# A recurrence, a post norm and two mixer layers re-ordered on one core

## The reference

```python
# first block
h = rms_norm(x, g_pre) * (1 + scale) + shift
q, k, v, g_att, u, g_lru, merge = split(h @ w_in)
y_a = (dilated_attention(q, k, v) * silu(g_att)) @ w_pa
u = causal_depthwise_conv(u, conv_w, conv_b)
# rg_lru: per feature, over the tokens t
r, i = sigmoid(u @ w_rg + b_rg), sigmoid(u @ w_ig + b_ig)   # 64 x 64 blocks
log_a = -8 * r * softplus(-lru_lambda); a = exp(log_a)
h_t = a * h_{t-1} + sqrt(-expm1(2 * log_a)) * (i * u)
y_b = (h * silu(g_lru)) @ w_pb
out = (gate_a * y_a + gate_b * y_b) @ w_o
x = x + gate * rms_norm(out, g_post)
# second block, for l in 0, 1: context ctx (256 tokens) and x (512 tokens)
hc, hx = modulate(rms_norm(ctx)), modulate(rms_norm(x))
a_val, a_gate, q, k, v, u, sv, bg, cg, xin = split(hx @ w_in[l])   # 10 parts of 256
y_a = silu(layer_norm(depthwise_conv31(a_val * sigmoid(a_gate))))
y_b = rms_norm((softmax(q1 k1) - lam * softmax(q2 k2)) v)   # 4 heads, keys of ctx and x
y_c = gelu(u) * (w_s @ layer_norm(gelu(sv)))
y_d = bg * depthwise_conv3(cg * xin)
x = x + gate * concat(y_a, y_b, y_c, y_d) @ w_out[l]
x = x + gate * relu(modulate(rms_norm(x)) @ w1)**2 @ w2
# layer 0 does all of this for ctx too
```

## Time and profile before

| | us |
|---|---|
| median of 3 runs (2217.7 to 2224.73) | 2219.04 |
| the profiled execution's own time | 2221.63 |
| its span in the trace | 2219.8 |
| TensorE busy | 2067.8 (93%) |
| VectorE busy | 1271.8 (57%) |
| ScalarE busy | 797.8 (36%) |
| GpSimd busy | 88.4 (4%) |
| TensorE's mean granted clock | 0.977 |

### The profile page before, as it was taken

How to read it: one execution, slowest core, us unless ns; L and a number is a source line. 1 busy time by engine, 2 the same in 40 slices (tenths; PEclk the granted TensorE clock), 3 DMA queues, 4 the chain that set the end, 5 groups by cost and what they waited for, 6 DMA issues and landing times.

```text
span 2219.8 us, 26153 instructions
## 1 busy us (share of the span) xinstructions
PE 2067.8 (93%) x11000; PEld 1756.8 (79%) x11000; DVE 1271.8 (57%) x1674; ACT 797.8 (36%) x1105; POOL 88.4 (4%) x89
## 2 busy tenths in 40 slices
PE   5999999998999898899999999999888889999998
PEld 5978777776777787788888888888777677888886
DVE  7465765756755695736645455464558555343343
ACT  4433334475243255424212121131525533232231
POOL 0000000000050000011000000001200000000001
PEclk9999999999998999999999999999999999999999
DMA  8533523522422531112323332232342212222222
GB/s 296 204 142 114 202 83 116 182 88 97 188 78 94 159 82 61 67 58 95 126 95 114 107 114 102 102 136 86 114 140 77 76 67 76 95 95 95 95 97 75
DMA packets 52821, 249.17 MB, mean 112 GB/s; under 512 B 6016, under 2 KB 10256, under 8 KB 34272
## 3 DMA queue, kind: packets, MB, share of 16 engines
q1 hardware_dynamic: 50816, 242.41, 31.6%
q0 software_dynamic: 592, 2.46, 0.3%
q10 hardware_dynamic: 1296, 2.63, 0.3%
HBM read 235.41 MB, written 12.06 MB: 111 GB/s over the span
## 4 chain that ended last, share of the span: by engine, by line
PE 74%; DVE 12%; ACT 7%; issue 4%; DMA 2%; POOL 0%; SPq 0%; ACTq 0%; DVEq 0%; POOLq 0%
PE banks L1707 62%; ACT whi_f L1829 2%; DVE small L1265 1%; DVE wlo_f L2011 1%; PE banks L607 1%; PE banks L616 1%; PE banks L1730 1%; PE banks L1731 1%; PE banks L1732 1%; PE banks L496 1%; DVE aconv L1177 1%; DVE prob L1285 1%; DMA mvr<-in_mst 1%; DVE mvr L2031 1%; PE banks L487 1%
## 5 line engine op out<-in xcount | busy, mean ns | idle before, releaser
L1707 PE MATMUL banks<-hxh,whi_f 128*128 128x512 f32 x1440 | 587.2, 408 | 47.8 <-DVE hxl L2050 14.9
L1707 PE MATMUL banks<-hxh,wlo_f 128*128 128x512 f32 x1440 | 571.2, 397 | 0.0
L1707 PE MATMUL banks<-hxl,whi_f 128*128 128x512 f32 x1440 | 570.6, 396 | 0.0
L2011 DVE TENSOR_TENSOR wlo_f<-raw_f,whi_f 128x2048 fp32r<-128x2048 f32 x133 | 305.7, 2298 | 215.0 <-ACT whi_f L1829 214.9
L1829 ACT ACTIVATE whi_f<-raw_f 128x2048 fp32r<-128x2048 f32 x133 | 253.8, 1908 | 310.3 <-PE banks L1707 291.7
L1707 PEld LDWEIGHTS banks<-hxh,whi_f 128*128 128x128 f32 x1440 | 275.1, 191 | 112.6 <-issue 42.9
L1707 PEld LDWEIGHTS banks<-hxh,wlo_f 128*128 128x128 f32 x1440 | 274.7, 191 | 60.1
L1707 PEld LDWEIGHTS banks<-hxl,whi_f 128*128 128x128 f32 x1440 | 275.3, 191 | 58.1 <-issue 1.9
L1707 PE MATMUL banks<-fxh,whi_f 128*128 128x512 f32 x512 | 202.5, 396 | 2.2 <-DVE cT L1395 1.1
L1395 DVE SCALAR_TENSOR_TENSOR xT<-banks,small,xT 128x512 f32<-128x512 f32 x80 | 59.5, 750 | 252.4 <-PE banks L1707 252.3
L1707 PE MATMUL banks<-fxh,wlo_f 128*128 128x512 f32 x512 | 201.3, 393 | 0.0
(11 more groups left out here) (316 smaller groups left out, 3170.9 us busy)
## 6 DMA issues: line engine op xcount, KB each, us to landing
raw_f<-in_wst SPq DMA_DIRECT2D x133, 1024.0 KB, 4.9
mvr<-in_mst SPq DMA_DIRECT2D x120, 512.0 KB, 5.8
stack<-qk_parts SPq DMA_DIRECT2D x48, 192.0 KB, 6.9
x_kept<-xT SPq DMA_DIRECT2D x2, 2048.0 KB, 8.6
raw_f<-in_wst SPq DMA_DIRECT2D x8, 384.0 KB, 6.0
xT<-x_kept SPq DMA_DIRECT2D x2, 1536.0 KB, 8.8
qk_parts<-qk_h SPq DMA_DIRECT2D x3, 768.0 KB, 3.4
qk_parts<-qk_l SPq DMA_DIRECT2D x3, 768.0 KB, 4.9
```

Source lines behind the costliest of these rows:

```text
L1707: last = pe.matmul(o, w[:, k, c, :], r[part][:, k, :], start=(k == order[0] and w is wh and part == 0), stop=(k == order[-1] and w is wl))
L2011: dve.tensor_tensor(wlo[r][:], raw[r][:], whi[n % 2 if n > N_FIRST else n][:].bitcast(F32), ALU.subtract).then_inc(w_lo, 1)
```

## The change

Recurrence: the result of tile j is written straight into `uc`, in the new token order, so that `bh` and `bl` are plain copies; they are made one pass later, `bh` between exp and sqrt, `bl` (`recurrence_low`) before VectorE waits for sqrt. Post norm: the split of chunk C_L + 1 moves behind the norm's root and inverse; GpSimd's adds for `n_mix[0]` go, and TensorE sums each of the eight squared tiles by itself (`tile_sums`), among the 32 context steps. Layers: the first stack of each layer is filled from `qk_h` and `qk_l` in SBUF by 16 transfers instead of from DRAM; `Y_ORDER`, the places of the rotations, of the convolution's taps and of several splits move; the context norm of layer 1 is begun in the last feed-forward chunk; accumulators are waited for one at a time; the y tiles wait tile by tile for their buffer (`hx_free`).

```diff
-Y_ORDER = (4, 5, 6, 7, 0, 1, 2, 3)
+Y_ORDER = (4, 5, 0, 1, 6, 7, 2, 3)
...
+                        if i == 0:
                             pe.wait_ge(acc_free[c], n)
-                        if k == 0 and c == 0:
-                            pe.wait_ge(acc_free[1], n)
-                        last = step(n, j % 2, k, c, own, at=lambda r: ctx_acc[:, c, :] if r[2] else acc[:, c, 0:T])
+                        if i == 0 and c == 0 and l == 0:
+                            pe.wait_ge(ctx_out, j - 5)
+                        last = step(n, j % 2, k, c, own, order, lambda r: ctx_acc[:, c, :] if r[2] else acc[:, c, 0:T])
...
-                 between={(0, 0): lambda: o_turned(0), (0, 2): lambda: o_turned(1)}, order=Y_ORDER)
+                 between={(0, 7): lambda: o_turned(0), (0, 2): lambda: o_turned(1)}, order=Y_ORDER)
...
+                if j > 2:
+                    high(j - 3)
...
-                    for k in range(KT):
-                        act.wait_ge(acc_free[k % 2], base - 4 + k // 2 + 1)
-                        norm_square(SC, cT, nsqc, k)
-                if j == 1 and l:
-                    norm_root(SC, c_mix[1])
+                    for k in range(4):
+                        norm_high(SC, c_mix[1], hch, k, mod_shift(0, k, 1))
...
-            square_o(0)
             upto(p.mean)
+            act.wait_ge(m_cen, l + 1)
+            act.activation(sqm[:, :, 0:wx], yca[:, :, 0:wx], ACT.Square).then_inc(m_sq, 1)
             act.wait_ge(sv_cen, l + 1)
...
-            act.wait_ge(m_cen, l + 1)
-            act.activation(sqm[:, :, 0:wx], yca[:, :, 0:wx], ACT.Square).then_inc(m_sq, 1)
+            square_o(0)
...
+                if i < 4:
+                    act.wait_ge(hx_free, 4 * l + i + 1)
+                else:
+                    act.wait_ge(acc_ready[1], base + N_WIN)
...
-            act.wait_ge(acc_ready[1], base + N_WIN)
             last = p.units - 1
-            if not two:
-                scaled(last)
-                square_o(1)
...
+            y_high(5)
             split(base + N_WIN + 1)
+            y_high(6)
+            y_high(7)
...
+                            if two:
+                                norm_square(SC, cT, nsqm, 2 * i + c)
...
+                for c in range(2):
+                    act.wait_ge(acc_free[c], n + 1)
+                    norm_square(SC, cT, nsqm, KT - 2 + c)
...
+                norm_root(SC, c_mix[1])
...
+                if j == 0 and l:
+                    for k in range(KT - 1):
+                        norm_scale(SC, c_mix[1], cT, k, coef[0][:, 2 * k + 1:2 * k + 2])
                 if j == 2:
-                    if l:
-                        for k in range(KT):
-                            conv(1)
-                            norm_scale(SC, c_mix[1], cT, k, coef[0][:, 2 * k + 1:2 * k + 2])
-                    else:
-                        conv(13)
+                    conv(13 if two else 11)
                 if j > 2:
                     rotate(j - 3)
+                    if j == 4:
+                        split(n + 1)
                     low(j - 3)
-                    conv(7 if two else 9)
-                split(n + 2)
+                    conv((7, 9)[j - 3] if two else 11)
+                if j != 3:
+                    split(n + 2)
...
+                    due[0] = n + 2
+            due = [None]
+            def weights_due():
+                if due[0] is not None:
+                    split(due[0])
+                due[0] = None
...
                 maxima(v0)
                 for v in range(v0, v1):
                     if v + 1 < v1:
                         maxima(v + 1)
+                    weights_due()
                     combine(v)
-                    conv(count)
+                    if v0 == 0:
+                        conv(3 if v < more else 2)
                     if v in late:
                         late[v]()
-            run(0, p.cut, 3)
+            run(0, p.cut, CONV_STEPS - taps[0] - 2 * p.cut)
...
+            dve.wait_ge(gelus, 2 * l + 1)
+            link(dve.tensor_scalar(sv_mean[:, 0:nj], sv_sum[:, 0:nj], 1.0 / GW, None, ALU.mult))
+            dve.tensor_tensor(svn[:, 0:nj, :], svn[:, 0:nj, :], by_row(sv_mean), ALU.subtract).then_inc(sv_cen, 1)
+            weights_due()
...
-            for i in range(4):
-                y_low(i)
+            y_low(0)
+            y_low(1)
+            upto(89)
+            y_low(2)
+            y_low(3)
...
+            y_low(5)
             split(base + N_WIN + 1)
+            y_low(6)
+            y_low(7)
...
+                if b == 0:
                     sync.wait_ge(x_kept, 16 * (l + 1))
                     sync.wait_ge(SX.low, KT * (n_mix[l].m + 1))
                     sync.wait_ge(SC.scaled, KT * (c_mix[l].m + 1))
+                for part, src in enumerate((qk_h[b], qk_l[b])):
+                    sync.wait_ge((qk_hi, qk_lo)[part], 2 * l + b + 1)
+                    for i in range(4):
+                        if STACKED[b][i] == part:
+                            for e in range(2):
+                                sync.dma_start(stack[0][32 * i:32 * i + 32, 2 * b + e, 0:w].bitcast(F32),
+                                               src[32 * e:32 * e + 32, 0, 0:w].bitcast(F32)).then_inc(stacked[0], 16)
+                    sync.dma_start(qk_dram[l][2 * b + part, :, :, 0:w].rearrange("c p t -> p c t"), src[:, :, 0:w].bitcast(F32)
+                                   ).then_inc(qk_kept[b], 16)
...
-                    load_stack(l, 0)
...
             add_square(SX, n_post, nsq, 6)
-            add_squares(SX, n_mix[0], nsq2)
             for l in range(L2):
                 if l:
-                    add_squares(SX, n_mix[1], nsq3)
-                    add_squares(SC, c_mix[1], nsqc)
+                    for k in range(1, KT - 1):
+                        add_square(SX, n_mix[1], nsq3, k)
+                        add_square(SC, c_mix[1], nsqm, k)
...
+            def tile_sums(k):
+                pe.wait_ge(SX.squared, KT * n_mix[0].i + k + 1)
+                for j in range(SX.nj):
+                    last = pe.matmul(SX.st[:, j:j + 1], nsq2[:, k, j * P:(j + 1) * P], ones[:, 0:1],
+                                     start=(k == 0 and j == 0), stop=(k == KT - 1), skip_group_check=True)
+                if k == KT - 1:
+                    last.then_inc(SX.summed, 1)
...
-                for k in range(KT):
+            sums_at = (13, 15, 16, 18, 19, 21, 22, 24)
+            for s in range(4 * KT):
+                j, c, k = s // (2 * KT), s // KT % 2, s % KT
+                if s % (2 * KT) == 0:
+                    weights(C_L + j)
+                if s in (0, KT):
+                    pe.wait_ge(acc_free[c], C_L)
+                if s == 3:
+                    norm_spread(SX, n_post)
+                if s in sums_at:
+                    tile_sums(sums_at.index(s))
+                if s == 27:
+                    norm_spread(SX, n_mix[0])
+                if j == 0:
                     wait_low(SC, c_mix[0], k)
-                    step(C_L, 0, k, c, [(*hc, T, TC)])
-                    if (c, k) == (0, 1):
...
-            norm_sums(SX, n_mix[0], nsq2)
-            norm_spread(SX, n_mix[0])
+                step(C_L + j, j, k, c, [(*hc, T + TC * j, TC)])
...
+                if j:
+                    act.wait_ge(lru_out, j)
                 act.activation(a_, r_, ACT.Exp, scale=nsp[:, j:j + 1]).then_inc(lru_ta, 1)
                 if j + 2 < N_MRG:
                     act.dma_start(wgate[:, j % 2, :], gst[j + 2]).then_inc(g_loaded[j % 2], 16)
+                if j:
+                    act.activation(tile(bh, j - 1), tile(uc, j - 1), ACT.Copy).then_inc(lru_hi, 1)
                 act.wait_ge(lru_z, j + 1)
                 act.activation(z_, z_, ACT.Sqrt).then_inc(lru_sq, 1)
-                act.wait_ge(lru_out, j + 1)
-                act.activation(by_residue(tile(bh, j)), in_order(x_), ACT.Copy).then_inc(lru_hi, 1)
             merged(N_MRG - 1)
+            act.wait_ge(lru_out, N_MRG)
+            act.activation(tile(bh, N_MRG - 1), tile(uc, N_MRG - 1), ACT.Copy).then_inc(lru_hi, 1)
             for j in range(N_PA):
...
+            def recurrence_low(j):
+                dve.wait_ge(lru_hi, j + 1)
+                dve.tensor_tensor(tile(bl, j), tile(uc, j), tile(bh, j).bitcast(F32), ALU.subtract
+                                  ).then_inc(lru_lo, 1)
             for j in range(N_MRG):
                 if j:
                     split(C_MRG + j + 1)
+                dve.wait_ge(lru_ri, 2 * j + 2)
+                link(dve.tensor_tensor(x_, i_, tile(uc, j), ALU.mult))
                 dve.wait_ge(lru_ta, 2 * j + 2)
                 link(dve.tensor_tensor(z_, a_, a_, ALU.mult))
                 dve.scalar_tensor_tensor(z_, z_, 1.0, tau, ALU.add, ALU.mult).then_inc(lru_z, 1)
-                link(dve.tensor_tensor(x_, i_, tile(uc, j), ALU.mult))
+                if j:
+                    recurrence_low(j - 1)
```

(8 more changed lines are left out.)

138 lines of the change are left out of this document (71 added, 67 removed).

## The result

Four runs of the changed kernel took 2181.31 us (2178.68 to 2183.21), against 2220.93 for the kernel before beside them: a ratio of 0.9831, 95% interval 0.981 to 0.9851. The profiled execution took 2182.12 us.

A forecast was written before the change was run, and what follows sets the result against it. TensorE, busy 2067.8 of 2219.8 us, was taken as the bound, losing time to long waits and half clock behind them. Terms 14.1 + 7.4 + 14.3 + 26.5 = 62.3 us; from 2221.63 that gives 2159.3, forecast 2159, range 2144 to 2182.

The forecast's parts named there:

- the single rivals and something of two together: High end 2182: waits back in mixers (2175, chance 0.15); ScalarE still pacing (2173) or stack not early (2172), together 0.12.
- Recurrence, 14.1 forecast: ScalarE's pass loses its 2.81 us wait before the bh copy; 11.1 us of TensorE waits and 3 of slow clock go.
- First norm, 7.4 forecast: Post norm and context chunks: sums by tile among the steps save 5 us, and 2.4 of clock comes back behind.
- the 4.6 saved: First norm: a tail of 12.1 us goes, eight sums at 0.94 us each add 7.5.
- My lower bound of 0: First norm: sums stall on each squared tile and eat the gain; bounds 0 to 11 us.
- half of 5.7: Stretch 666.2 to 688.6 ran at 0.70; if half the lost 5.7 us of clock returns, 2.4 more.
- Layer 0's loop, 1.0 forecast: Accumulators released singly shorten svn, ug and cx waits; the split between maxima and combine gives some back: 1.0 us net.
- The rival of waits inside the mixers: Waits come back in loops and mean parts, with a 2.29 us split in the chain: 16 us lost, 2175; chance 0.15.
- The start of layer 0, 7.8 forecast: Direct transfers remove stack and vnat waits and slow clock, 8.9 us, less 1.1 for a weight split before the first maxima.
- Layer 0's mean part and mixers' end, 5.5 forecast: The 4.4 us wait for sqm goes, part returns at the spread: 3.3; short waits at the mixers' end give 2.2.
- Layer 1, 26.5 forecast: Context norm 8.1 us, stack and first scores 5.9, loop 5.5, mean part 1.7, y tiles 5.3.
- the slower side: Several short waits hold TensorE at the lower clock through the mixers; both loops at half clock give 2269; chance 0.03.

The follow-up runs named there:

- eight profiles: Profiled executions with the changed kernel's sums by tile among the context steps, that code the same in all; matmul 1824 to 2016 took 51.2 to 54.5 us.
- one-group: Changed kernel with all eight sums by tile together ahead of step 24, not spread among the steps; matmul 1824 to 2016 took 51.3 us.
- two-sum kernels: Changed kernel with six of the eight sums by tile left out; matmul 1824 to 1920 took 23.3 us against 28.7 to 32.1 with all sums.
- second profile of the changed kernel: Changed kernel run again unedited, beside the kernel before; median 2182.23 us, ratio 0.982.
- ten profiles: Profiled executions with the changed kernel's order in layer 0's loop not edited; that loop (matmul 2208 to 2400) took 69.5 to 72.6 us.
- three such swaps: Changed kernel with split back before next maxima, first maxima ahead of a split, and roots of y_a's variance first; 2163.86 us, 0.975 of the kernel before.
- kernel with four adds: Changed kernel with GpSimd adding squares 1 to 4 to square 0 and four sums ahead of step 24; matmul 1824 to 2016 took 51.3 us.

## Why the prediction was right or wrong

The direction was right, and so was the recurrence. The sum was too large: 62.3 us forecast, 39.6 measured. The step that failed first is the price of the new work in the first norm; the second is that short waits inside the mixers were counted without the clock behind them. Of the 22.5 us or so that are missing by the table, 9.0 lie in the first norm, 6.4 in layer 0's loop and mean part and 8.4 in layer 1, less 1.3 that the recurrence gave over its forecast. That the time still lies inside the range, 0.7 us from its end, is owed to the range being wide enough for "the single rivals and something of two together".

- **Recurrence, 14.1 forecast, 15.4 measured.** Right by its steps: the 2.81 went, TensorE set the pace, all of the 11.1 us of waits and the half clock behind went. I had taken at least 0.5 too little for the copy (1.14 to 0.62).
- **First norm, 7.4 forecast, -1.6 measured (between 1.7 and -1.7 over the eight profiles).** The step that failed is "eight such matmuls took 1.87, so 0.94 each, 7.5 in all". The row was misread twice. Its x8 are records, two for each of these matmuls, so the 1.87 us are one sum of four matmuls and not two; and it was taken at the lower clock, 0.50. The kernel before has the same work at full clock as well:

```profile
645.00 1.05 PE L1675 MATMUL banks<-consts,nsq 128*128 128x1 f32 x8 [0.31 <-POOL nsq L1604]
```

```profile
644.90:646.90 2.00, 1.90 (x17) 1.00 0.58 123
666.20:669.80 3.60, 3.56 (x16) 0.50 1.03 437
```

  The two errors cancel, so 0.94 is by luck the price at full clock (0.95 to 1.05 measured). But most of the sums ran at the lower one: 1.70 each, and by rows 6 read rightly eight of them would be 15.0 us, which turns the 4.6 saved into some 3 lost. To this comes what I did not look for, namely what the new work does to the clock: once the sums had begun, the level fell, and the steps between them took longer too. Over 25 us the clock was 0.6, some 10 us lost. My lower bound of 0, sums stalling on the squares, had another mechanism and was not low enough. Of the clock in layer 0's first chunk I expected 2.4 back ("half of 5.7" would be 2.9), and 2.3 came (22.4 against 24.7). That the sums bring the fall is shown by the one-group and two-sum kernels and by the second profile of the changed kernel.
- **Layer 0's loop, 1.0 forecast, -3.8 measured (-2.3 to -5.4 over ten profiles).** I had the mechanism ("the split between maxima and combine gives some back") and its size wrong: the new waits of 1.9 us for `prob` add little to the idle time, but 3.2 us of busy time came with them as the clock went from 1.00 to 0.95. The rival of waits inside the mixers was right here and in layer 1. With the split back where it was, about 2.4 us return; what holds the clock down for the rest is not settled.
- **The start of layer 0, 7.8 forecast and measured, but for other reasons.** I gave it all to the direct transfers; they are worth 3.7 of it. The wait of 5.8 had two parts: through DRAM again it is 3.6, so other edits had taken the rest. That the sum of this term came out is luck.
- **Layer 0's mean part and mixers' end, 5.5 forecast, 3.9 measured (2.6 to 3.9).** The wait of 4.4 for sqm went; the wait at the spread that came back was 2.2, where I had left 1.1.
- **Layer 1, 26.5 forecast, 18.1 measured.** The context norm gave 5.8 instead of 8.1, and 2.7 of the missing come and go between runs of the same code, so the term was about right. The stack and loop fell short because the first maxima wait behind a weight split: I had 3.3 for that, and it cost a wait of 3.6 with some 3 us of clock behind it (1626 to 1636 at 0.60 and 0.50). The wait for the spread was 4.3, where I had 2.0 coming back. The y tiles gave 4.0 of 5.3.
- **The clock.** I wrote against the slower side that "the level fell only behind waits of 3.6 us and more". The trace of the kernel before does not say so. In layer 1's loop it stands at half behind the svn wait of 2.5 us and again behind the wait of 2.7 for `prob`:

```profile
1683.30:1686.60 3.30, 3.30 (x11) 0.50 1.04 254
1724.30:1727.60 3.30, 3.30 (x12) 0.50 0.00 0
```

  The slower side did not come: the loops' clock is 0.97 in layer 0 and 0.94 in layer 1. But in smaller measure its mechanism explains much of what is missing: 25 us at 0.6 in the first norm, and short stretches at half behind waits of 1.9 to 3.6 us.

## What to carry to other kernels

Where short work that keeps TensorE little occupied, such as sums of one column, is to be put among dense matmuls, price it at both clocks, and the neighbours too, and see first what a row counts and at which clock it was taken: here records were taken for matmuls and half clock for full. When a long wait goes, read the order list for the next bulk operation (here a weight split of 2.3 us) ahead of a short one that TensorE waits for, and put the short one first: three such swaps, each seen in a wait row, gave 18 us together (16 by stages), nearly half as much as the whole change. Take one more profile of the same code before a difference of a stretch is put down to an edit: layer 0's loop alone moved by 3 us. Credit a gain to one of several edits only after undoing that one: the transfers that I took for the cause of 7.8 us were worth 3.7.

## What the runs showed of the hardware

TensorE's granted clock fell to its lower level while TensorE was never idle. In the one-group kernel it was busy 9.00 of 9.00 us at 1.00 up to 642, the last 1.9 us of them in sums of one column, and 2.00 of 2.00 us at 0.65 in the next two; in the second profile of the changed kernel it was busy 6.40 of 6.40 us at 1.00 with three sums among the steps, then 16.80 of 16.80 us at 0.50. Eight sums gave 0.58 over 17 us, two gave 0.93 over 24 us with more idle time. I had expected only idle time to do this. How long the lower level lasts differs from run to run of the same code, and the stretch (1824 to 1920) moved with it between 28.7 and 32.1 us. The same holds for layer 0's loop: with nearly the same idle time it took 69.6 us at a clock of 0.98 and 71.0 at 0.95. GpSimd's adds beside VectorE's slowed them from 0.68 to 1.0 us once more, in the kernel with four adds as in the one before. Each of a sum's four matmuls stands in these traces as two records, so a sum reads x8.
